# Two transformer blocks on one core: the first projections of four norms start before the norm is known, and GpSimd transfers make some of the weights' remainders

## The reference

```python
for l in range(2):                                   # first block
    h = rms_norm(x, g) * (1 + scale1) + shift1
    x = x + g1 * token_mixer(h)                      # latent attention, block attention, convolution, gates
    h = rms_norm(x, g) * (1 + scale2) + shift2
    a, b = split(causal_depthwise_conv(h @ w_up))    # w_up: 1024 x 5632, 3 taps
    x = x + g2 * ((silu(a) * b) @ w_down)
for l in range(2):                                   # second block, beside 256 context tokens
    x = ffn_half_step(x)                             # norm, scale and shift, swiglu, width 2752
    x = x + gate * mixer(x)                          # l = 0: Fourier and chunk mixing; l = 1: attention
    x = ffn_half_step(x)
return rms_norm(x, g_final)
```

## Time and profile before

| | |
|---|---|
| median of 3 runs | 2626.76 us (2626.3 to 2628.7) |
| profiled execution | 2623.43 us, its span 2621.6 us |
| PE busy | 2581.4 us, 98% |
| DVE, ACT, GpSimd busy | 67%, 41%, 3% |
| granted clock of PE, mean | 0.995 |
| ring transfers | 822 of 512 KB, 3.5 us from issue to landing (median) |
| DMA | 168 GB/s over the span |

### The profile page before, as it was taken

How to read it: one execution, slowest core, us unless ns; L and a number is a source line. 1 busy time by engine, 2 the same in 40 slices (tenths; PEclk the granted TensorE clock), 3 DMA queues, 4 the chain that set the end, 5 groups by cost and what they waited for, 6 DMA issues and landing times.

```text
span 2621.6 us, 38515 instructions
## 1 busy us (share of the span) xinstructions
PE 2581.4 (98%) x15546; PEld 2229.8 (85%) x15546; DVE 1747.9 (67%) x2815; ACT 1086.5 (41%) x1685; POOL 67.9 (3%) x59
## 2 busy tenths in 40 slices
PE   8999999999999999999999999999999999999998
PEld 4789889877898899978888888888898888887997
DVE  5678777656787777757674458665677765387554
ACT  3546366535453675422223334222333222356442
POOL 0000000000000000100001010000000000100000
PEclk9999999999999999999999999999999999999999
DMA  8663467655634676464452213544435544231553
GB/s 329 229 194 111 148 208 248 220 196 196 198 108 172 221 244 217 151 215 178 161 193 91 98 62 137 185 153 145 145 122 193 187 170 163 82 121 65 179 184 113
DMA packets 120880, 441.13 MB, mean 168 GB/s; under 512 B 13312, under 2 KB 14720, under 8 KB 120192
## 3 DMA queue, kind: packets, MB, share of 16 engines
q1 hardware_dynamic: 120704, 438.68, 48.9%
HBM read 437.58 MB, written 1.05 MB: 167 GB/s over the span
## 4 chain that ended last, share of the span: by engine, by line
PE 93%; DVE 3%; ACT 2%; DMA 1%; issue 0%; SPq 0%; DVEq 0%; ACTq 0%
PE ps L657 24%; PE ps L658 24%; PE ps L659 24%; PE ps L661 14%; PE ps L654 5%; PE ps L655 3%; DMA ring<-stream 1%; DVE rests L1918 1%; PE ps L669 1%; ACT heads L1379 0%; DVE rs L1978 0%; DVE h_split L2034 0%; DVE rt L2025 0%; DVE rs L2018 0%; DVE rt L2182 0%
## 5 line engine op out<-in xcount | busy, mean ns | idle before, releaser
L657 PE MATMUL ps<-h_split,heads 128*128 128x256 f32 (+1 forms) x3192 | 1028.8, 322 | 7.1 <-DVE rests L1918 3.5
L658 PE MATMUL ps<-h_split,heads 128*128 128x256 f32 (+1 forms) x3192 | 1014.9, 318 | 0.0
L659 PE MATMUL ps<-h_split,rests 128*128 128x256 f32 (+1 forms) x3192 | 1014.6, 318 | 0.0
L1918 DVE TENSOR_TENSOR rests<-ring,heads 128x1024 fp32r<-128x1024 f32 x548 | 665.7, 1231 | 189.9 <-ACT heads L1379 182.9
L1379 ACT ACTIVATE heads<-ring 128x1024 fp32r<-128x1024 f32 x548 | 568.2, 1056 | 471.9 <-DMA ring<-stream 218.6
L657 PEld LDWEIGHTS ps<-h_split,heads 128*128 128x128 f32 x3192 | 610.0, 191 | 81.4 <-ACT rt L1558 15.1
L658 PEld LDWEIGHTS ps<-h_split,heads 128*128 128x128 f32 x3192 | 610.4, 191 | 42.3 <-issue 1.9
L659 PEld LDWEIGHTS ps<-h_split,rests 128*128 128x128 f32 x3192 | 610.1, 191 | 40.2
L1945 DVE SCALAR_TENSOR_TENSOR qt<-ring,silu_rows 128x1024 f32<-128x1024 f32 x240 | 286.5, 1231 | 5.2 <-issue 1.8
L657 PE MATMUL ps<-hid_split,heads 128*128 128x512 f32 (+1 forms) x660 | 236.3, 358 | 0.0
L659 PE MATMUL ps<-hid_split,rests 128*128 128x512 f32 (+1 forms) x660 | 235.7, 357 | 0.0
(11 more groups left out here) (229 smaller groups left out, 2425.2 us busy)
## 6 DMA issues: line engine op xcount, KB each, us to landing
ring<-stream SPq DMA_DIRECT2D x822, 512.0 KB, 3.5
consts<-constants SPq DMA_DIRECT2D x1, 1728.0 KB, 10.9
x_sb<-x_in SPq DMA_DIRECT2D x1, 1024.0 KB, 11.4
x_sb<-ctx_in SPq DMA_DIRECT2D x1, 1024.0 KB, 4.8
silu_rows<-rows_in SPq DMA_DIRECT2D x1, 1024.0 KB, 7.7
out<-area SPq DMA_DIRECT2D x1, 1024.0 KB, 4.8
consts<-constants SPq DMA_DIRECT2D x1, 704.0 KB, 9.3
cols<-columns SPq DMA_DIRECT2D x1, 538.5 KB, 10.1
```

Of the source, the lines that this page charges most:

```text
L657: nc.tensor.matmul(out, lhsT[0], rhs[0], start=first, stop=False)
L658: nc.tensor.matmul(out, lhsT[0], rhs[1], start=False, stop=False)
L659: ins = nc.tensor.matmul(out, lhsT[1], rhs[0], start=False, stop=last)
L1918: nc.vector.tensor_tensor(rests[:, u % RING, :], ring[:, u % RING, :], as_f32(heads[:, n % HEADS_RING, :]), ALU.subtract)\
```

## The change

1. At the four norms the quad no longer waits for the norm. As each tile of x is updated, ACT rounds x times its factor into `pre_heads`, and DVE makes the remainder `pre_rests`. The shift is carried as two more columns (rounded part and remainder) of `pre_heads`, so that a product has 258 columns. Once the reciprocal is known, DVE multiplies the four output tiles by it from PSUM and adds up the two shift columns as an offset per output channel, which later steps of ACT add. The squares' sum is made behind k = 0 of the quad, and the filler is dropped. The other projections still take normalised tiles, which are made as before. The splits move: `prepare` ahead of the last square, one at tile 5 (`PRE_SPLIT`), and one in place of two ahead of pair 0.
2. For odd units of `up_0` and `up_1` (44 of 88) DVE makes no remainder. ACT writes the negated heads over the ring slot, and GpSimd starts a transfer that reads the unit from HBM again and adds it to the slot. PE waits for the transfer's landing. GpSimd issues them behind the norm's `sums`.

```diff
+def is_added(name, u):
+
+    return name is not None and name.startswith("up_") and u % 2 == 1
...
+                if at == 0 and u in added_so_far:
+                    pe.wait_ge(scalar_done, A.at(("heads", split_index[u])))
+                    pe.wait_ge(rests_added[slot], 16 * added_so_far[u])
+                elif at == 0 and split:
                     pe.wait_ge(vector_done, V.at(("rest", split_index[u])))
                 elif at == 0:
                     pe.wait_ge(weights_landed[slot], 16 * (u // RING + 1))
...
+            def linear_quad_scaled(what, name, p):
+
+                outs = [o for c in range(2) for o in take_two((*what, c), SEQ + 2)]
+                before = T.unit
+                for k in range(KD):
+                    pe.wait_ge(vector_done, V.at((p, "pre", k)))
+                    for e in range(4):
+                        w, unit = weights(name, k, e)
+                        done = (*what, e // 2) if k == KD - 1 and e % 2 else None
+                        nc.tensor.matmul(outs[e], w[0], pre_heads[:, k, :], start=k == 0, stop=False)
+                        nc.tensor.matmul(outs[e][:, 0:SEQ], w[0], pre_rests[:, k, :], start=False, stop=False)
+                        ins = nc.tensor.matmul(outs[e], w[1], pre_heads[:, k, :], start=False, stop=k == KD - 1)
+                        if unit is not None:
+                            T.found[unit] = (T.n + 1, T.unit)
+                        if done is not None or unit is not None:
+                            ins.then_inc(tensor_done, T.mark(done))
+                    if k == 0:
+                        for tile in range(SUMMED - 1, KD):
+                            mean_square(p, SEQ, tile)
+                        T.found[(p, "ms")] = (T.n, before)
+                return once(lambda k: pe.wait_ge(vector_done, V.at((p, "h", k))))
...
+            def add_weights(name):
+
+                for u in added:
+                    if first_name(u) == name:
+                        pool.wait_ge(scalar_done, A.at(("minus heads", split_index[u])))
+                        pool.dma_start(rests[:, u % RING, :], stream[u, :, :], accum_op=ALU.add)\
+                          .then_inc(rests_added[u % RING], 16)
...
+                add_weights(f"up_{l}")
...
+                if u in added_so_far:
+                    own()
+                    nc.scalar.activation(rests[:, u % RING, :], as_f32(heads[:, n % HEADS_RING, :]), ACT.Copy, scale=-1.0)\
+                      .then_inc(scalar_done, A.mark(("minus heads", n)))
...
+                if pre is not None:
+                    act.wait_ge(vector_done, V.at((p, "adapted")))
+                    nc.scalar.activation(pre_heads[:, :, SEQ:SEQ + 1], shifts, ACT.Copy)\
+                      .then_inc(scalar_done, A.mark((p, "shift head")))
                 for k in range(KD):
+                    if pre is not None and k == KD - 1:
+                        prepare(p)
                     if updated is not None:
-                        act.wait_ge(vector_done, after(V, updated(k)))
+                        act.wait_ge(vector_done, after(V, updated(k), pre is None or k < KD - 1))
                     nc.scalar.activation(squared(T_, k).rearrange("p (v t) -> p v t", v=T_ // SEQ),
                                          x[:, 0:T_ // SEQ, k, :], ACT.Square)\
                       .then_inc(scalar_done, A.mark((p, "sq", k)))
+                    if pre is not None:
+                        nc.scalar.activation(pre_heads[:, k, 0:SEQ], x[:, 0, k, :], ACT.Identity, scale=amod[:, pre, k, 0:1])\
+                          .then_inc(scalar_done, A.mark((p, "pre head", k)))
...
+                def scaled_pair(j):
+
+                    act.wait_ge(vector_done, after(V, (p, "scaled", j), False))
+                    for ab in range(2):
+                        nc.scalar.activation(z[:, j, ab, FFN_TAPS - 1:], z[:, j, ab, FFN_TAPS - 1:], ACT.Identity,
+                                             bias=offsets[:, j, ab:ab + 1]).then_inc(scalar_done, A.mark())
+                    own()
+                    for ab in range(2):
+                        nc.scalar.activation(zc[:, j, ab, :], z[:, j, ab, FFN_TAPS - 1:], ACT.Identity,
+                                             scale=c(w0 + (2 * 2 + ab) * FJ, j), bias=c(b0 + ab * FJ, j))\
+                          .then_inc(scalar_done, A.mark((p, "z", j) if ab else None))
...
+                if u in added_so_far:
+                    return
...
+            def pre_rest(p, slot, k):
+
+                dve.wait_ge(scalar_done, A.at((p, "pre head", k)))
+                nc.vector.scalar_tensor_tensor(out=pre_rests[:, k, :], in0=x[:, 0, k, :], scalar=amod[:, slot, k, 0:1],
+                                               in1=as_f32(pre_heads[:, k, 0:SEQ]), op0=ALU.mult, op1=ALU.subtract)\
+                  .then_inc(vector_done, V.mark((p, "pre", k)))
...
+            def scaled_tiles(g, c, out, name):
+
+                banks, offset = scaled_banks(g)
+                dve.wait_ge(tensor_done, after(T, g, False))
+                nc.vector.tensor_reduce(offsets[:, c, :], offset, AX.X, ALU.add).then_inc(vector_done, V.mark())
+                nc.vector.tensor_tensor(out, banks, rs[:, 0:SEQ].rearrange("p (a t) -> p a t", a=1).to_broadcast([P, 2, SEQ]),
+                                        ALU.mult).then_inc(vector_done, V.mark(name))
+                V.found[("read", g)] = V.found[name]
...
+            def norm(p, T_, slot, shift, gain=None, begin=None, pre=False):
+
+                if pre:
+                    prepare(p)
+                    pre_rest(p, slot, KD - 1)
+
+                dve.wait_ge(scalar_done, after(A, ("read", (p, "ms")), False))
...
+                    if pre and k - 1 == PRE_SPLIT:
+                        next_split()
...
+                            if scaled is None:
+                                next_split()
+                            else:
+                                scaled(0)
+                                scaled(1)
...
+                    for c in range(2):
+                        scaled_tiles((p, "lat", c), c, lat[:, 2 * c:2 * c + 2, :], (p, "lat scaled", c))
```

More of the change, by code:

```diff
@@ L106 @@
 CONTEXT_PAIR = 10
+PRE_SPLIT = 5
 LAST_TWO_SUMS = 4
@@ L520, in build @@
         weights_landed = [sem(f"weights_landed{s}") for s in range(RING)]
+        rests_added = [sem(f"rests_added{s}") for s in range(RING)]
         output_stored = sem("output_stored")
@@ L545, in first_name @@
             return (blocks[u * UB] or (None,))[0]
+        added = [u for u in split_units if is_added(first_name(u), u)]
+        added_so_far = {u: sum(a % RING == u % RING for a in added[:i + 1]) for i, u in enumerate(added)}
         own_left = [u for u in range(units) if is_own(first_name(u))]
@@ L843, in hook, with ffn @@
                     pending.append(group)
-            def ffn(p, up, down, T_, ready, then=None, order=(0, 1), total=None, beside=None):
+            def ffn(p, up, down, T_, then=None, order=(0, 1), total=None, beside=None):
                 shared = T_ == SEQ
@@ L1401, in norm @@
                         next_split()
-                    if rows_first is None and k == 2:
-                        prepare(p)
-                    act.wait_ge(vector_done, after(V, (p, "hn", k), rows_first is None))
+                    if pre is not None and k == PRE_SPLIT:
+                        next_split()
+                    act.wait_ge(vector_done, after(V, (p, "hn", k), False))
                     for v in range(halves):
@@ L1588, in each_pair @@
                             next_split()
+                        if j == 0 and T_ == TOK:
                             next_split()
@@ L1606, in gate @@
                     lo = max(q for q in los if q <= j)
+                    if T_ == SEQ and j < 2:
+                        act.wait_ge(vector_done, after(V, (p, "scaled", j), False))
+                        nc.scalar.activation(sg[:, j, 0:SEQ], rt[:, j, 0:SEQ], ACT.Silu, bias=offsets[:, j, 0:1])\
+                          .then_inc(scalar_done, A.mark((p, "si", j)))
+                        return
                     g = (p, "up", j) if T_ == SEQ or half_tile(up, j) else (p, "gate", j)
@@ L1644, in _ @@
                 for c in range(3):
-                    copy_pair(lat[:, 2 * c:2 * c + 2, :].rearrange("p a t -> p (a t)"), (p, "lat", c), apart=c < 2)
+                    if l > 0 and c < 2:
+                        act.wait_ge(vector_done, after(V, (p, "lat scaled", c)))
+                        for e in range(2):
+                            nc.scalar.activation(lat[:, 2 * c + e, :], lat[:, 2 * c + e, :], ACT.Identity,
+                                                 bias=offsets[:, c, e:e + 1]).then_inc(scalar_done, A.mark())
+                    else:
+                        copy_pair(lat[:, 2 * c:2 * c + 2, :].rearrange("p a t -> p (a t)"), (p, "lat", c), apart=c < 2)
                     own()
@@ L1967, in hook, with adapt @@
```

(24 more changed lines are left out.)

115 lines of the change are left out of this document (69 added, 46 removed).

## The result

The changed kernel takes 2737.6 us (median of 4 runs, 2731.5 to 2743.8) against 2626.5 for the kernel before beside it: a ratio of 1.0423, interval 1.0408 to 1.0439. That is slower by 111 us, where 28 were forecast, and outside the range of 2622 to 2698. The profiled execution took 2733.3 us, its span 2731.6.

What follows compares the result with a forecast made beforehand. The prediction took PE (TensorE), busy 98% of the span, as the bound. Transfers cost +27 us in `up_0` and +7 in `up_1`, norms gave -4.5 and -1.7: +28 us, forecast 2655 us, range 2622 to 2698.

Steps and rivals of the forecast that it cites:

- X: Added units in both up stages: time from the negated heads to PE's release, taken as 6.0 us, upper bound 9.
- the transfer is dear: Rival for the added units: X of 8 and more, +66 us and up, 2692 to 2712; chance 0.22.
- an estimate of 3.2 us: Skill's rule for a GpSimd transfer: 2.0 us plus bytes over 436 GB/s; not used in the sum.
- The formula: Two pairs take 9.3 + X = 15.3 us in `up_0`, 13.5 in `up_1`, against 12.9; eight steps cost 19 and 5.
- the term that I put at nothing: PE's clock behind its waits: the forecast's sum holds no term for it.
- The entry into each stage: Start of the up stages: 4.5 us later at pair 4 plus 3.2 at unit 115 in `up_0`; about even in `up_1`.
- Unit 115: First added unit of `up_0`: there at 343.4 where PE wants it at 340.15, costing 3.2 us.
- The fourth: Norm `f2` of the last block: a gain of 4.5 us.
- the first two: Norms ahead of `up_0` and in layer 1's mixer: gains of 1.3 and 1.7 us.
- the third: Norm ahead of `up_1`: a gain of 1.3 us, ACT's first pairs being the bound.
- my 8.8: All four norms without the transfers: a gain of 4.5 + 1.7 + 2 x 1.3 = 8.8 us.
- the wait of 2.8 us in layer 1's mixer: Sixth projection of layer 1's mixer: a new wait of PE for DVE's remainder, 2.8 us, leaving that norm's gain at 1.7.

Runs made afterwards that it cites:

- e4: The changed kernel with plain transfers in place of accumulating ones; 2679.5 us, ratio 1.0209.
- e6: The changed kernel with transfers in every other pair only, 22 units in place of 44; 2723.7 us, ratio 1.0376.
- e12: The changed kernel with two filler products ahead of each of the 44 waits for an added unit; 2722.5 us, ratio 1.0367.
- e1: The changed kernel with the norms' part only, no unit added by a transfer; 2628.6 us, ratio 1.0014.
- e9: e1 with four fillers ahead of the fifth pair's wait in each up stage and two at layer 1's sixth projection; 2618.5 us, ratio 0.9975.
- e8: The changed kernel with three filler products ahead of each of the 44 waits for an added unit; 2730.1 us, ratio 1.0390.
- e7: e1 with the split of two units moved from ahead of the last tile's square to behind it; 2628.6 us, ratio 1.0014.
- e2: The kernel before with the accumulating transfers alone, without the norms' change; 2732.2 us, ratio 1.0404.

## Why the prediction was wrong

**X, the first step that failed.** I took 6.0 us from the negated heads to PE's release, as the median landing of SP's transfers plus one instruction of GpSimd. Measured in the first stage (window 346 to 560) and the second (930 to 1110):

```profile
rests<-stream POOLq DMA_DIRECT2D x20, 512.0 KB, 7.2
```

```profile
rests<-stream POOLq DMA_DIRECT2D x21, 512.0 KB, 7.8
```

GpSimd starts the issue 0.36 us behind the negated copy (median), and the landing is counted from there, so the medians of X are 7.6 and 8.1. In `up_0`, from the fifth pair on, PE waits for every other pair only (4, 6, 8 and so on), and for these the mean of X is 8.0; in `up_1` it is 7.9 over all. My rival "the transfer is dear", with X of 8 and more, named about that size, but of its two reasons only the adding is shown (2.2 us by e4), and loaded engines don't explain it (e6). Its price was too low as well, 2692 to 2712: my sum gives +66 for an X of 8, and 111 were measured. The Trainium skill (DMA: Bandwidth & Descriptors, Anatomy of one DMA, SWDGE path) gave an estimate of 3.2 us; neither the plain transfer of this kernel (5.3) nor the adding one (7.5) agrees.

**The formula held, as far as the chain goes.** One step of it, from pair 4 to pair 6 of `up_0`, in rows of ACT, GpSimd and PE:

```profile
403.95 1.07 ACT L1430 ACTIVATE heads<-ring 128x1024 fp32r<-128x1024 f32 x1
405.05 1.06 ACT L1434 ACTIVATE rests<-heads 128x1024 fp32r<-128x1024 f32 x1
```

```profile
406.46 0.86 POOL L1370 DMA_DIRECT2D rests<-stream  x1 [14.96 <-ACT rests L1434]
```

```profile
413.27 0.40 PE L678 MATMUL ps<-h_split,heads 128*128 128x256 f32 x1 [4.00 <-DMA rests<-stream]
```

On the mean of the eight steps PE's pair takes 7.5 us from its first product to its last, ACT's copies begin 1.7 later and take 2.2, X is 8.0, and PE starts 0.1 behind the landing: 19.6 in all. With X measured, my formula gives 9.3 + 8.0 = 17.3 us in `up_0` and 7.5 + 7.9 = 15.4 in `up_1`, against 12.9 before: 8 x 4.4 + 8 x 2.5 = 55 us, where I had 24.

**TensorE's clock, the term that I put at nothing.** I counted waits as waits. But behind most of the waits of several microseconds here the products come at 1.2 GHz. The issues' steps of 19.9 and 16.8 give 8 x (7.0 + 3.9) = 87 us, 32 more than the formula. In `up_0` the pair's 7.5 us would be 5.6 at the full pace, which is 15 of the 32. In `up_1` four awaited units took 3.9 to 4.3 us each instead of 2.8, which is 5 more; the other 12 I can't split. The fillers gave back 15 us in e12, with some waiting and filling of its own. The length of a wait doesn't decide alone. Of these two in `up_1` the longer is followed by five microseconds at 1.00 and the shorter by five at 0.71:

```profile
981.86 0.36 PE L678 MATMUL ps<-h_split,heads 128*128 128x256 f32 x1 [3.25 <-DMA rests<-stream]
982.05 0.28 PE L679 MATMUL ps<-h_split,heads 128*128 128x256 f32 x1
982.17 0.28 PE L680 MATMUL ps<-h_split,rests 128*128 128x256 f32 x1
```

```profile
1021.09 0.55 PE L678 MATMUL ps<-h_split,heads 128*128 128x256 f32 x1 [2.80 <-DMA rests<-stream]
1021.45 0.41 PE L679 MATMUL ps<-h_split,heads 128*128 128x256 f32 x1
```

In the norms the same mistake cost 10 us (e1 to e9). I took away the filler as pure gain, and behind the two kinds of wait that stood there in its place, 2.6 us at the sixth projection and 4.3 where 1.6 stood, the granted clock was 0.68 and 0.50 over five microseconds in e1.

**The entry into each stage.** The fifth pair (my pair 4) starts at 393.99, 51.5 us after the stage before ended at 342.48; before it was 34.2. I had 4.5 + 3.2 = 7.7 us for it, and it was 17. Unit 115 alone holds the quad back by 6.96 us, where I had 3.2: I let GpSimd issue it at 337.4, as before behind its sums, but the sums wait for ACT's squares, and ACT's copy and negated copy stand ahead of the sixth square.

```profile
338.03 1.05 ACT L1430 ACTIVATE heads<-ring 128x1024 fp32r<-128x1024 f32 x1
339.12 1.06 ACT L1434 ACTIVATE rests<-heads 128x1024 fp32r<-128x1024 f32 x1
340.24 0.42 ACT L1450 ACTIVATE sq<-x_sb 128x256 f32<-128x256 f32 x1
```

```profile
341.86 1.01 POOL L1370 DMA_DIRECT2D rests<-stream  x1 [0.32 <-POOL sq L1361]
```

So the sum was done late, the issue came at 341.86, and PE's first product followed 7.6 us behind it, at 349.44. That is a moved step whose queue I had not followed. In `up_1` the entry, which I had as even, costs about 9 us: its fifth pair's added unit starts at 981.86, 46.5 us into the stage, where the same unit began 37.2 us in before.

The parts make up the stages: 56 + 17 = 73 us in `up_0` and 31 + 9 = 40 in `up_1`, where A to B lost 70 and C to D 41. Of the 83 us between the forecast's 28 and the measured 111, then, X is 31, the steps beyond the formula some 30, the entries 18, and the rest mostly the norms.

**The norms.** The fourth gained 3.4 us of the 4.5 forecast. For the others e9, at a clock of 0.996, shows 1.4 for the first two (forecast 3.0) and for the third a loss of 0.6 (forecast a gain of 1.3), which is within what unchanged stretches differ by. A cause that fits, though e7 didn't show it as time won back, is the double split of e1: the last square 1.5 us late for PE, and the chain of the first pairs some 2 us later than I had it (the fifth pair starts 35.1 us behind the quad's start of 340.17 in e9, 34.2 us in before, 32.9 in the forecast). In all, the medians give e9 a gain of 7 us (interval 4 to 9) against my 8.8. But beside the transfers the norms gave nothing that can be told from zero: the change is at 1.0423 (1.0408 to 1.0439), e2 without them at 1.0404 (1.0386 to 1.0422).

**What was right.** That the kernel gets slower, and that PE's waits for a transfer are most in `up_0`; but they came once in two pairs there and were 3.5 to 8.9 us long from the fifth pair on, not 2 to 4, and 41 of the 110 us are in `up_1`, not nearly none. Right too were the fourth norm as a gain and the wait of 2.8 us in layer 1's mixer (2.59). That DVE's 54 us of freed time gain nothing by themselves was argued only; no run tests it.

**What stays open.** Why the median of an adding landing was 5.6 us in e8's first stage and 6.7 to 8.1 in every other kernel that adds 512 KB. How much of e12's step is chain and how much filler. What decides whether the clock falls at a wait of about 3 us. A longer ring, which would let the copies for an added unit begin earlier, wasn't tried.

## What to carry to other kernels

Price a transfer that takes over an engine's work by its latency in the loop that waits for it, not by its bandwidth: with a ring of four `heads` places, everything between the release of one place and the use of the next counts in full, and with half as many transfers the step was as long (20.2 us against 19.9). A wait of PE of some microseconds can cost more than itself, because the products behind it may come at half speed (0.50 granted behind the 4.27 us of e1); a few products of constants in it can be worth more than the reordering that shortens it, and removing filler is not free. When a copy is put in front of other work on an engine, follow all that waits for that work, GpSimd's queue too.

## What the hardware showed that I had not expected

- A transfer from GpSimd that adds lands 2.2 us later than a plain one of the same 512 KB (7.5 against 5.3, counted from the start of the issue), and its issue takes 0.87 us against 0.53. With half as many of them in flight (e6) the landing was no shorter, 7.8.
- Over the five microseconds behind PE's waits of 4.27 us (e1) and 8.85 us (changed kernel) the granted clock was 0.50, that is 1.2 GHz; behind one of 3.25 us it was 1.00 and behind one of 2.80 us 0.71 (both in the changed kernel). With four filler products in front of the first of these waits the clock stayed at 1.00, 2.4 GHz, and fillers at three places (ten products) were worth 10 us of 2628.
